# A split-precision transformer block on one core: the order of the weight products within a chunk

## The chip, the cores and the metric

The kernel runs on one NeuronCore of a Trainium2 chip. The metric is the device time of one execution in microseconds. Three executions of the kernel before took 2243.55, 2243.20 and 2241.29 us; their median is 2243.2 us.

## What is computed

Two transformer-like layers in sequence, over 256 tokens (the first with 16 meta tokens put ahead, 272 in all) and a model width of 2048, all in float32. Shortened from the reference:

```
# first block
h    = rms_norm(x, norm_g);  proj = h @ w_in            # 2048 x 12368 columns
y_a  = sparse attention (indexer, top-k) * silu(z_a)
y_b  = rms_norm(gated recurrence)       * silu(z_b)
x    = x + (sigmoid(gates) * (y @ w_branch)) summed over 2 branches @ w_out
# second block, modulated by mod = silu(c) @ ada_w + ada_b
h    = modulate(rmsnorm(x, norm1_g)); p = h @ w_in_2
y    = [neighbourhood attention, Fourier mix, long convolutions]
x    = x + g1 * (y @ w_out_2)
x    = x + g2 * ((gelu(conv(h2 @ w_gate)) * (h2 @ w_up)) @ w_down)
return rmsnorm(x, final_norm_g)
```

Nearly all the arithmetic is activations times large weight matrices (w_in, w_branch, w_out, w_in_2, w_out_2, ffn_w_up, ffn_w_down), each weight used once.

## The kernel before

The weights stream from memory into four buffers `raw`. ScalarE writes their upper part in fp32r (`whi`, line 561), VectorE the remainder (`wlo = raw - whi`, line 1104). Activations are split in the same way into a high and a low plane: `phi`/`plo` for most phases, `r_hi`/`r_lo` for phase FB, `y_hi`/`y_lo` for E, `c_hi`/`c_lo` for G and H, `o_hi`/`o_lo` for OA, `dhi`/`dlo` for M0 and M1. A full-precision product is then the sum of three fp32r products on TensorE, called a triple here: whi with the high plane, whi with the low plane, wlo with the high plane. Each of the three is one matmul instruction with a weight load (LDWEIGHTS) of its own.

The work is a list of units, each 256 output columns (for M0 and M1, all 1024 of a half), in phases FB, QB, IB, QI, K, KA, QA, VA, ZB, ZA, GA, GB, E, F, G, H, IH, IF, J, IQ, OA, OB, L, M0, M1. A unit is cut into chunks of 512 rows of the weight (four row tiles of 128, index `k4`; `kt` counts them over the unit), four chunks to most units. The function `chunk(c)` of TensorE (lines 1767 to 1830) issues one chunk's products; it waits once, at its start, for the chunk's `wlo` (semaphore `split_lo`), at the start of a unit for the banks to be evacuated (`gemm_free`), and its last product alone signals `mm`, on which ScalarE (which refills `whi`) and the evacuations wait. Unit u sums in banks 2p and 2p+1 of PSUM, p = u mod 2. There are three kinds:

- weights stationary, activations moving (lines 1785 to 1807; most phases): output columns on the partitions, in two halves `h` of 128, one bank each; the loop is h outside, k4 inside, then the triple. So twelve products in a row go to one bank, then twelve to the other. The moving operand has 256 columns, or 272 in FB, IB, KA, VA and the first half of K. In phase K the second half has only 16 stationary columns.
- DN, phases M0 and M1 (lines 1808 to 1819): activations stationary, 512 weight columns moving, one row tile to a chunk, four banks (two token halves `t`, two column halves `nb`); the bank changes after every triple.
- the rest, N2, phases H and J (lines 1820 to 1829): activations stationary, 256 weight columns moving, k4 outside, then t, then the triple; the bank changes after every triple.

Between chunks TensorE runs smaller work of the block (attention, recurrence, convolutions, transposes, the ada products), written out by hand at given chunk numbers.

Of the kernel before, what the change touches and what calls it, by code (L numbers as in the profile page):

```python
# [7 lines left out]
KT = D // 128  # L8
SEQ = 256
META = 16  # L10
T = META + SEQ
# [4 lines left out]
UC = 256  # L16
# [24 lines left out]
U0, NU, UNITS, C0, CHUNK = {}, {}, [], [], []  # L41
# [123 lines left out]
def program(nc, A, out):  # L165
# [5 lines left out]
    with ctx:  # L171
        top = [MEM]

        def at(name, shape, offset, dt=F32):
            return nc.alloc_sbuf_tensor_at(name, shape, dt, offset=4 * offset)
# [7 lines left out]
        def S(name):  # L183
            if name not in sems:
                sems[name] = ctx.enter_context(nc.semaphore(name))
            return sems[name]
# [17 lines left out]
        dhi = at("dhi", [128, 8, 256], base + 24576, F32R)  # L204
        dlo = at("dlo", [128, 8, 256], base + 26624, F32R)
# [11 lines left out]
        ps = [ctx.enter_context(nc.psum_tensor(f"ps{i}", [128, 512], F32)) for i in range(8)]  # L217
# [1546 lines left out]
        def _(pe):  # L1764
            mm = nc.tensor.matmul

            def chunk(c):

                u, q = CHUNK[c]
                name, kind, i = UNITS[u]  # L1770
                p = u % 2
                pe.wait_ge(S("split_lo"), c + 1)
                if kind == "DN":
                    j = u - U0["M0"]
                    if q == 0:
                        pe.wait_ge(S("dn_lo"), j + 1)
                elif q == 0 and u >= 2:

                    pe.wait_ge(S(f"gemm_free{p}"), (u - p) // 2)
                wh, wl = whi[c % 4], wlo[c % 4]  # L1780
                xh, xl = {"E": (y_hi, y_lo), "G": (c_hi, c_lo), "H": (c_hi, c_lo)}.get(name, (phi, plo))
                if name == "FB":
                    xh, xl = r_hi, r_lo
                if name == "OA":
                    xh, xl = o_hi[:, 4 * q:4 * q + 4, :], o_lo[q]
                if kind in ("Tall", "Tx", "T", "T8", "K", "BR"):
                    cc = {"Tall": slice(0, T), "Tx": slice(META, T), "K": slice(0, T)}.get(kind, slice(0, 256))
                    n = 144 if kind == "K" else UC
                    for h in range(2):
                        m = 16 if kind == "K" and h == 1 else 128  # L1790
                        if kind == "K" and h == 1:
                            cc = slice(META, T)
                        w = cc.stop - cc.start
                        b = 256 * (q // 2) if kind == "BR" else 0
                        o = ps[2 * p + h][0:m, b:b + w]
                        for k4 in range(4):
                            kt = 4 * q + k4
                            k = slice(n * k4 + 128 * h, n * k4 + 128 * h + m)
                            if u == 0 and h == 0:
                                pe.wait_ge(S("raw_lo"), kt + 1)  # L1800
                            st, en = kt == 0, c + 1 == C0[u + 1] and k4 == 3
                            if kind == "BR":
                                st, en = kt % 8 == 0, kt % 8 == 7
                            xk, yk = xh[:, k4 if name == "OA" else kt, cc], xl[:, k4 if name == "OA" else kt, cc]
                            mm(o, wh[:, k], xk, start=st, stop=False)  # L1805
                            mm(o, wh[:, k], yk, start=False, stop=False)  # L1806
                            l = mm(o, wl[:, k], xk, start=False, stop=en)  # L1807
                elif kind == "DN":
                    kd = 4 * p + q
                    for t in range(2):  # L1810
                        for nb in range(2):
                            o = ps[(4 if name == "M0" else 0) + 2 * t + nb][:, :]
                            k = slice(512 * nb, 512 * nb + 512)
                            xk = dhi[:, kd, 128 * t:128 * t + 128]
                            yk = dlo[:, kd, 128 * t:128 * t + 128]
                            st, en = i == 0 and q == 0, i == 10 and q == 3
                            mm(o, xk, wh[:, k], start=st, stop=False)  # L1817
                            mm(o, yk, wh[:, k], start=False, stop=False)  # L1818
                            l = mm(o, xk, wl[:, k], start=False, stop=en)  # L1819
                else:  # L1820
                    for k4 in range(4):
                        kt = 4 * q + k4
                        k = slice(UC * k4, UC * k4 + UC)
                        for t in range(2):
                            tt = slice(128 * t, 128 * t + 128)
                            o = ps[2 * p + t][:, 0:UC]
                            mm(o, xh[:, kt, tt], wh[:, k], start=kt == 0, stop=False)  # L1827
                            mm(o, xl[:, kt, tt], wh[:, k], start=False, stop=False)  # L1828
                            l = mm(o, xh[:, kt, tt], wl[:, k], start=False, stop=kt == KT - 1)  # L1829
                l.then_inc(S("mm"), 1)  # L1830

            def ada_tile(n):
# [107 lines left out]
            def attention(s):  # L1940

                c, odd = (s - S_NK) // 2, (s - S_NK) % 2
                if 1 <= c <= 13 and not odd:
                    chunk, w, _, _, _, pm = rope_of(c - 1)
                    if c == 1:
                        pe.wait_ge(S("rope_in"), 48)
                    if c - 1 < NNORM:
                        pe.wait_ge(S("nk_normed"), c)
                    if c >= 2:
                        pe.wait_ge(S("nk_turned"), c - 1)  # L1950
                    mm(ps[5][:, 0:w], pm, chunk, start=True, stop=True).then_inc(S("nk_rot"), 1)
# [49 lines left out]
            for c in slots("FB", "GB"):  # L2001
# [8 lines left out]
                u, q = CHUNK[c]  # L2010
                if (u, q) in TURN_AT:
                    to_tokens(TURN_AT[u, q])
                if u == U0["K"] + 1 and q == 0:
                    p = U0["K"] % 2
                    pe.wait_ge(S(f"gemm_free{p}"), evacuated(U0["K"], p))
                    pe.wait_ge(S("vt_tok"), 8)
                    for t in range(2):
                        l = nc.tensor.transpose(ps[6][:, 16 * t:16 * t + 16], wiT[0:16, 128 * t:128 * t + 128], ident[0:16, 0:16])
                    l.then_inc(S("wi_tp"), 1)
                recurrence(c)  # L2020
                if c == S_QN:
# [4 lines left out]
                    for j in range(16):  # L2026
                        l = mm(ps[6][:, j:j + 1], sqq[j // 4][:, 128 * (j % 4):128 * (j % 4) + 128], mean1[:, 0:1], start=True, stop=True)
# [174 lines left out]
            for c in slots("E", "OB"):  # L2202
                u, q = CHUNK[c]
                name, _, i = UNITS[u]
# [24 lines left out]
            for c in slots("L", "M1"):  # L2229
# [8 lines left out]
                kt = c - START["L"] - 8  # L2238
                if 0 <= kt < 16:
# [3 lines left out]
                    for t in range(2):  # L2243
                        l = nc.tensor.transpose(ps[4 + kt % 2][:, 128 * t:128 * t + 128], x1T[:, kt, 128 * t:128 * t + 128], ident[:, :])
# [129 lines left out]
```

## Time and profile before

| | |
|---|---|
| executions, us | 2243.55, 2243.20, 2241.29 (median 2243.2) |
| profiled execution, us | 2243.54 |
| its span, first to last instruction, us | 2241.7 |
| mean granted TensorE clock | 0.993 |
| busy: TensorE, its weight loads | 2186.1 us (98%), 2034.5 us (91%) |
| busy: VectorE, ScalarE | 1453.4 us (65%), 1028.9 us (46%) |
| matmuls and weight loads | 16534 each |

All from one profiled execution. Matmuls overlap in the pipeline: a record of 0.28 us stands every 0.12 us, so the time that one product costs is the distance from its start to the next one's start, and not its duration; busy time is the time that at least one is under way. In a window, the count in brackets includes those that started ahead of the window and end in it.

### The profile page before, as it was taken

The page shows a single profiled execution, that of the slowest core. Times are in us where ns is not written, and L with a number is a line of the kernel's source. Part 1 is how long each engine was busy: PE and PEld are TensorE (multiplying, and loading weights), DVE is VectorE, ACT ScalarE, POOL GpSimd, SP SyncE. Part 2 cuts the span into 40 slices and gives each one's busy share as a digit, 9 for nine tenths or more (in the row PEclk, how much of TensorE's full clock was granted, in tenths as well). Part 3 has the DMA queues.
Part 4 walks back from the last instruction along what each step waited for, and adds up shares of the span by engine and source line. Part 5 has one row for each costly group of instructions (what it writes and reads, how often), then busy time and mean ns, then how long its engine had stood idle before and what let it go on. Part 6 is the DMA issues. An engine that isn't in the chain of part 4 may idle for free.

```text
span 2241.7 us, 37995 instructions
## 1 busy us (share of the span) xinstructions
PE 2186.1 (98%) x16534; PEld 2034.5 (91%) x16534; DVE 1453.4 (65%) x1796; ACT 1028.9 (46%) x1394; POOL 6.2 (0%) x10
## 2 busy tenths in 40 slices
PE   7999999999999999999999999979999999999996
PEld 7989989878999999998888999979999999998885
DVE  7656546656757697696665677776666665555654
ACT  6453334334455555454433454454444443444453
POOL 0000000000000000000000000000000000000000
PEclk9999999999999999999999999989999999999998
DMA  9755655655447978786565756746676675555552
GB/s 318 248 197 192 190 190 172 205 194 176 145 150 256 314 232 266 252 279 221 181 206 155 239 165 206 244 166 233 223 237 233 228 233 188 182 190 199 189 191 92
DMA packets 344260, 469.55 MB, mean 209 GB/s; under 512 B 20445, under 2 KB 318301, under 8 KB 331102
## 3 DMA queue, kind: packets, MB, share of 16 engines
q1 hardware_dynamic: 344094, 467.12, 62.9%
q8 instruction: 130, 2.13, 0.4%
q14 instruction: 36, 0.29, 0.0%
HBM read 465.00 MB, written 2.10 MB: 208 GB/s over the span
## 4 chain that ended last, share of the span: by engine, by line
PE 94%; DVE 3%; ACT 2%; DMA 1%; issue 0%; SPq 0%; DVEq 0%; ACTq 0%
PE ps L1805 23%; PE ps L1807 22%; PE ps L1806 22%; PE ps L1819 4%; PE ps L1817 4%; PE ps L1818 4%; PE ps L1899 1%; PE ps L1828 1%; PE ps L1829 1%; PE ps L1827 1%; PE ps L1841 1%; ACT whi L561 1%; DVE wlo L1104 1%; PE ps L2176 1%; PE ps L2109 1%; PE ps L2103 1%
## 5 line engine op out<-in xcount | busy, mean ns | idle before, releaser
L1104 DVE TENSOR_TENSOR wlo<-raw,whi 128x1024 fp32r<-128x1024 f32 (+1 forms) x668 | 815.1, 1222 | 734.9 <-ACT whi L561 733.1
L561 ACT ACTIVATE whi<-raw 128x1024 fp32r<-128x1024 f32 (+1 forms) x668 | 705.2, 1056 | 1138.4 <-PE ps L1807 933.6
L1805 PE MATMUL ps<-phi,whi 128*128 128x256 f32 (+2 forms) x3744 | 1080.5, 289 | 7.5 <-DVE plo L1561 6.7
L1806 PE MATMUL ps<-plo,whi 128*128 128x256 f32 (+2 forms) x3744 | 1056.1, 282 | 0.0
L1807 PE MATMUL ps<-phi,wlo 128*128 128x256 f32 (+2 forms) x3744 | 1055.7, 282 | 0.0
L1805 PEld LDWEIGHTS ps<-phi,whi 128*128 128x128 f32 (+1 forms) x3744 | 707.5, 189 | 40.9 <-issue 30.2
L1806 PEld LDWEIGHTS ps<-plo,whi 128*128 128x128 f32 (+1 forms) x3744 | 704.8, 188 | 7.2 <-issue 6.0
L1807 PEld LDWEIGHTS ps<-phi,wlo 128*128 128x128 f32 (+1 forms) x3744 | 708.2, 189 | 0.3
L1170 DVE SCALAR_TENSOR_TENSOR arena<-raw,cst,arena 128x1024 f32<-128x1024 f32 x120 | 153.6, 1280 | 3.5 <-DVE arena L1251 0.5
L1817 PE MATMUL ps<-whi,dhi 128*128 128x512 f32 x352 | 136.9, 389 | 0.0
L1819 PE MATMUL ps<-wlo,dhi 128*128 128x512 f32 x352 | 136.9, 389 | 0.0
L1818 PE MATMUL ps<-whi,dlo 128*128 128x512 f32 x352 | 136.9, 389 | 0.0
L1818 PEld LDWEIGHTS ps<-whi,dlo 128*128 128x128 f32 x352 | 66.1, 188 | 13.8
L1819 PEld LDWEIGHTS ps<-wlo,dhi 128*128 128x128 f32 x352 | 66.1, 188 | 13.7
L1817 PEld LDWEIGHTS ps<-whi,dhi 128*128 128x128 f32 x352 | 66.1, 188 | 13.6
L1805 PE MATMUL ps<-y_hi,whi 128*128 128x256 f32 x256 | 72.1, 282 | 0.0
L1806 PE MATMUL ps<-y_lo,whi 128*128 128x256 f32 x256 | 71.8, 280 | 0.0
L1807 PE MATMUL ps<-y_hi,wlo 128*128 128x256 f32 x256 | 71.6, 280 | 0.0
L1805 PE MATMUL ps<-r_hi,whi 128*128 128x272 f32 x128 | 38.8, 303 | 12.1 <-DVE wlo L1104 12.1
L1806 PEld LDWEIGHTS ps<-y_lo,whi 128*128 128x128 f32 x256 | 48.2, 188 | 0.0
L1807 PEld LDWEIGHTS ps<-y_hi,wlo 128*128 128x128 f32 x256 | 48.2, 188 | 0.0
L1805 PEld LDWEIGHTS ps<-y_hi,whi 128*128 128x128 f32 x256 | 48.0, 187 | 0.0
(347 smaller groups left out, 2324.4 us busy)
## 6 DMA issues: line engine op xcount, KB each, us to landing
raw<-w_in_dram SPq DMA_DIRECT2D x151, 1024.0 KB, 6.2
raw<-ada_w_dram SPq DMA_DIRECT2D x96, 1024.0 KB, 5.0
raw<-ffn_w_up_dram SPq DMA_DIRECT2D x88, 1024.0 KB, 5.1
raw<-ffn_w_down_dram SPq DMA_DIRECT2D x44, 1024.0 KB, 5.2
raw<-w_out_dram SPq DMA_DIRECT2D x32, 1024.0 KB, 5.7
raw<-w_branch_dram SPq DMA_DIRECT2D x16, 1024.0 KB, 6.5
arena<-xT_dram SPq DMA_DIRECT2D x4, 544.0 KB, 6.9
arena<-ctxT_dram SPq DMA_DIRECT2D x1, 2048.0 KB, 10.5
```

Source lines behind the costliest of these rows:

```text
L561: nc.scalar.activation(whi[c % 4][:, 0:w], src, ACT.Copy).then_inc(S("split_hi"), 1)
L1104: v.tensor_tensor(wlo[c % 4][:, 0:w], src, whi[c % 4][:, 0:w].bitcast(F32), ALU.subtract).then_inc(S("split_lo"), 1)
L1170: t = v.scalar_tensor_tensor(total, x, by, R(ADA_SUM[n - 1][half], 1024), ALU.mult, ALU.add)
L1805: mm(o, wh[:, k], xk, start=st, stop=False)
L1806: mm(o, wh[:, k], yk, start=False, stop=False)
L1807: l = mm(o, wl[:, k], xk, start=False, stop=en)
L1817: mm(o, xk, wh[:, k], start=st, stop=False)
L1818: mm(o, yk, wh[:, k], start=False, stop=False)
L1819: l = mm(o, xk, wl[:, k], start=False, stop=en)
L1827: mm(o, xh[:, kt, tt], wh[:, k], start=kt == 0, stop=False)
L1828: mm(o, xl[:, kt, tt], wh[:, k], start=False, stop=False)
L1829: l = mm(o, xh[:, kt, tt], wl[:, k], start=False, stop=kt == KT - 1)
```

## The change

In all three kinds, the loop over the banks becomes the innermost. For each row tile the first term of the triple (whi, high plane) is issued to every bank of the unit in turn, then the second term (whi, low plane) to every bank, then the third (wlo, high plane). No two products in a row write the same bank any more. The same products are issued with the same operands, each with its own weight load; in each bank the terms are added in the same order. The waits, the signal `mm` on the chunk's last product and the start and stop flags of each bank stay; for unit 0 the wait for `raw_lo` now stands ahead of six products of a row tile in place of three. In the first kind, terms one and two shared their stationary slice of `whi`; now no two neighbours share one, and instead the moving plane is the same in each pair (the two halves `h`). In DN neighbours that differ in `nb` alone now share the stationary tile. In N2 the moving slice of the weights is the same in each pair (the two `t`); before, terms one and two shared it.

```diff
--- before.py
+++ after.py
@@ -1783,50 +1783,40 @@
                     xh, xl = r_hi, r_lo
                 if name == "OA":
                     xh, xl = o_hi[:, 4 * q:4 * q + 4, :], o_lo[q]
+
                 if kind in ("Tall", "Tx", "T", "T8", "K", "BR"):
                     cc = {"Tall": slice(0, T), "Tx": slice(META, T), "K": slice(0, T)}.get(kind, slice(0, 256))
                     n = 144 if kind == "K" else UC
-                    for h in range(2):
-                        m = 16 if kind == "K" and h == 1 else 128
-                        if kind == "K" and h == 1:
-                            cc = slice(META, T)
-                        w = cc.stop - cc.start
-                        b = 256 * (q // 2) if kind == "BR" else 0
-                        o = ps[2 * p + h][0:m, b:b + w]
-                        for k4 in range(4):
-                            kt = 4 * q + k4
-                            k = slice(n * k4 + 128 * h, n * k4 + 128 * h + m)
-                            if u == 0 and h == 0:
-                                pe.wait_ge(S("raw_lo"), kt + 1)
-                            st, en = kt == 0, c + 1 == C0[u + 1] and k4 == 3
-                            if kind == "BR":
-                                st, en = kt % 8 == 0, kt % 8 == 7
-                            xk, yk = xh[:, k4 if name == "OA" else kt, cc], xl[:, k4 if name == "OA" else kt, cc]
-                            mm(o, wh[:, k], xk, start=st, stop=False)
-                            mm(o, wh[:, k], yk, start=False, stop=False)
-                            l = mm(o, wl[:, k], xk, start=False, stop=en)
+                    b = 256 * (q // 2) if kind == "BR" else 0
+                    for k4 in range(4):
+                        kt = 4 * q + k4
+                        if u == 0:
+                            pe.wait_ge(S("raw_lo"), kt + 1)
+                        st, en = kt == 0, c + 1 == C0[u + 1] and k4 == 3
+                        if kind == "BR":
+                            st, en = kt % 8 == 0, kt % 8 == 7
+                        xi = k4 if name == "OA" else kt
+                        for x, wx, first, last in ((xh, wh, st, False), (xl, wh, False, False), (xh, wl, False, en)):
+                            for h in range(2):
+                                m = 16 if kind == "K" and h == 1 else 128
+                                tt = slice(META, T) if kind == "K" and h == 1 else cc
+                                k = slice(n * k4 + 128 * h, n * k4 + 128 * h + m)
+                                l = mm(ps[2 * p + h][0:m, b:b + tt.stop - tt.start], wx[:, k], x[:, xi, tt], start=first, stop=last)
                 elif kind == "DN":
                     kd = 4 * p + q
-                    for t in range(2):
-                        for nb in range(2):
-                            o = ps[(4 if name == "M0" else 0) + 2 * t + nb][:, :]
-                            k = slice(512 * nb, 512 * nb + 512)
-                            xk = dhi[:, kd, 128 * t:128 * t + 128]
-                            yk = dlo[:, kd, 128 * t:128 * t + 128]
-                            st, en = i == 0 and q == 0, i == 10 and q == 3
-                            mm(o, xk, wh[:, k], start=st, stop=False)
-                            mm(o, yk, wh[:, k], start=False, stop=False)
-                            l = mm(o, xk, wl[:, k], start=False, stop=en)
+                    st, en = i == 0 and q == 0, i == 10 and q == 3
+                    for x, wx, first, last in ((dhi, wh, st, False), (dlo, wh, False, False), (dhi, wl, False, en)):
+                        for t in range(2):
+                            for nb in range(2):
+                                l = mm(ps[(4 if name == "M0" else 0) + 2 * t + nb][:, :], x[:, kd, 128 * t:128 * t + 128],
+                                       wx[:, 512 * nb:512 * nb + 512], start=first, stop=last)
                 else:
                     for k4 in range(4):
                         kt = 4 * q + k4
                         k = slice(UC * k4, UC * k4 + UC)
-                        for t in range(2):
-                            tt = slice(128 * t, 128 * t + 128)
-                            o = ps[2 * p + t][:, 0:UC]
-                            mm(o, xh[:, kt, tt], wh[:, k], start=kt == 0, stop=False)
-                            mm(o, xl[:, kt, tt], wh[:, k], start=False, stop=False)
-                            l = mm(o, xh[:, kt, tt], wl[:, k], start=False, stop=kt == KT - 1)
+                        for x, wx, first, last in ((xh, wh, kt == 0, False), (xl, wh, False, False), (xh, wl, False, kt == KT - 1)):
+                            for t in range(2):
+                                l = mm(ps[2 * p + t][:, 0:UC], x[:, kt, 128 * t:128 * t + 128], wx[:, k], start=first, stop=last)
                 l.then_inc(S("mm"), 1)
 
             def ada_tile(n):
```

## Rows read from the trace of the kernel before

**Rows 1.** The page: busy time by engine; granted clock in 40 slices.

```profile
PE 2186.1 (98%) x16534; PEld 2034.5 (91%) x16534; DVE 1453.4 (65%) x1796; ACT 1028.9 (46%) x1394; POOL 6.2 (0%) x10
...
PEclk9999999999999999999999999989999999999998
```

**Rows 2.** The page: the chain that ended last, by engine and by line.

```profile
PE 94%; DVE 3%; ACT 2%; DMA 1%; issue 0%; SPq 0%; DVEq 0%; ACTq 0%
PE ps L1805 23%; PE ps L1807 22%; PE ps L1806 22%; PE ps L1819 4%; PE ps L1817 4%; PE ps L1818 4%; PE ps L1899 1%; PE ps L1828 1%; PE ps L1829 1%; PE ps L1827 1%; PE ps L1841 1%; ACT whi L561 1%; DVE wlo L1104 1%; PE ps L2176 1%; PE ps L2109 1%; PE ps L2103 1%
```

**Rows 3.** Waits of TensorE, the longest: us in total, times, longest.

```profile
PE ps L1805 <- DVE wlo L1104: 12.1, 1, 12.1
```

**Rows 4.** Groups by line: xcount | busy us, mean ns | idle before.

```profile
L1805 PE MATMUL ps<-phi,whi 128*128 128x256 f32 (+2 forms) x3744 | 1080.5, 289 | 7.5 <-DVE plo L1561 6.7 <-DVE plo L1697 0.8
...
L1817 PE MATMUL ps<-whi,dhi 128*128 128x512 f32 x352 | 136.9, 389 | 0.0
...
L1805 PE MATMUL ps<-r_hi,whi 128*128 128x272 f32 x128 | 38.8, 303 | 12.1 <-DVE wlo L1104 12.1
...
L1827 PE MATMUL ps<-whi,c_hi 128*128 128x256 f32 x128 | 36.2, 283 | 0.0
```

**Rows 5.** Windows, TensorE alone: stretch, us, busy (xproducts), granted clock, DMA share, GB/s.

```profile
744.40:789.60 45.20, 45.20 (x386) 1.00 0.92 317
801.40:835.90 34.50, 34.50 (x290) 1.00 0.82 266
...
954.60:977.60 23.00, 23.00 (x194) 1.00 0.87 288
977.60:1023.70 46.10, 46.10 (x386) 1.00 0.84 280
1570.20:1831.40 261.20, 261.20 (x2210) 1.00 0.68 230
1985.40:2224.40 239.00, 239.00 (x1056) 1.00 0.50 174
```

**Rows 6.** Timeline, phase L: start us, duration; 24 products of one chunk, of which five.

```profile
1750.89 0.28 PE L1805 MATMUL ps<-phi,whi 128*128 128x256 f32 x1
1751.00 0.28 PE L1806 MATMUL ps<-plo,whi 128*128 128x256 f32 x1
1751.12 0.28 PE L1807 MATMUL ps<-phi,wlo 128*128 128x256 f32 x1
1751.24 0.28 PE L1805 MATMUL ps<-phi,whi 128*128 128x256 f32 x1
...
1753.73 0.28 PE L1805 MATMUL ps<-phi,whi 128*128 128x256 f32 x1
```

**Rows 7.** Timeline, phase J: first product of a chunk and what follows its 24th.

```profile
1151.98 0.28 PE L1827 MATMUL ps<-whi,phi 128*128 128x256 f32 x1
...
1154.82 0.59 PE L2109 MATMUL ps<-arena 128*128 128x512 f32 x1
```

**Rows 8.** Timeline, phase H: the bank changes at every L1827.

```profile
984.96 0.28 PE L1828 MATMUL ps<-whi,c_lo 128*128 128x256 f32 x1
985.08 0.28 PE L1829 MATMUL ps<-wlo,c_hi 128*128 128x256 f32 x1
985.20 0.28 PE L1827 MATMUL ps<-whi,c_hi 128*128 128x256 f32 x1
```

**Rows 9.** Timeline, phase M0: the bank changes at every L1817.

```profile
2051.55 0.39 PE L1818 MATMUL ps<-whi,dlo 128*128 128x512 f32 x1
2051.78 0.39 PE L1819 MATMUL ps<-wlo,dhi 128*128 128x512 f32 x1
2052.01 0.39 PE L1817 MATMUL ps<-whi,dhi 128*128 128x512 f32 x1
```

**Rows 10.** Timeline, the first products, at half clock.

```profile
12.92 0.43 PE L1805 MATMUL ps<-r_hi,whi 128*128 128x272 f32 x1
...
14.28 0.43 PE L1805 MATMUL ps<-r_hi,whi 128*128 128x272 f32 x1
```

## The prediction

> **What bounds the kernel.** First the page's busy times: TensorE is under way 98% of the span, VectorE 65%, ScalarE 46%, and the clock is granted in full in all but two of 40 slices [rows 1]. But a matmul record of 0.28 us stands every 0.12 us [rows 6], so 98% says only that a product is always in the pipe, not that the array is at its peak. Then the chain of waits: 94% of it is TensorE, and 82% the nine lines of `chunk` that the change rewrites [rows 2]. The longest wait of TensorE is its start, 12.1 us [rows 3]. So it's the distance from one product's start to the next that makes the time, and a nanosecond of it on all products counts in full. ScalarE and VectorE have slack of 54% and 35%: a TensorE faster by a few per cent would still be fed.
>
> How many products: phi as the moving operand has 3744 triples, FB 128, H 128 [rows 4]; G, OA and J have 128 each as H has, E 256, M0 and M1 together 352 [rows 4]. That is 4512 + 128 + 352 = 4992 triples, 14,976 products. 1200 of them have 272 columns (12 units of 96, and half of K), 1056 have 512, 48 are K's small ones, which leaves 12,672 of 256 columns.
>
> What one costs, from the windows (count less the two already under way at the window's start, one in M0/M1) [rows 5]:
> - L, units 8 to 30: 2208 in 261.2 us, 118.3 ns
> - E, first four units: 384 in 45.2 us, 117.7 ns; E, last three: 288 in 34.5 us, 119.8 ns, as good as 120
> - G: 192 in 23.0 us, 119.8 ns. H: 384 in 46.1 us, 120.1 ns
> - M0 and M1 (512 columns): 1055 in 239.0 us, 226.5 ns
>
> **What is there to gain.** H and M0 differ by 256 columns and 106.4 ns, so 0.416 ns a column, the array's 2.4 GHz; 256 columns are 106.5 ns, and each product carries 11.8 ns (L) to 13.6 ns (H) on top. In the first products, at the 1.2 GHz level, six of 272 columns take 1.36 us [rows 10], 0.833 ns a column, and nothing on top. Whatever the 12 to 14 ns are, they show only at full clock. The change helps if they are a stall of a product that adds to sums which its forerunner has just written.
>
> **The bank in the trace of before.** The old code has both cases side by side. In H the bank changes after each triple. The steps are: from term one to two and from two to three (same bank), 0.12 us; from term three to the next triple's first (another bank), 0.12 us [rows 8]; here three rows of 16 alike. A stall in the two same-bank steps would make the third one shorter. In M0 the same: 0.23 us within the bank and 0.23 us at the change [rows 9]. A buffer ahead of the array could smear such a stall over a triple; but G changes its bank after twelve products and H after three, with the same planes c_hi and c_lo: 119.8 and 120.1 ns [rows 5]. Were the bank to matter, H, with a third of its steps going to another bank, would be well below G. L and J give the same answer on phi and plo: one chunk of L is 24 products in 2.84 us (of 1750.89 to 1753.73) [rows 6], one chunk of J with the change at each third product is 24 in 2.84 us (1151.98 to 1154.82) [rows 7]: 118.3 ns both. So I take the bank's worth as zero.
>
> **The change part by part.**
> - Instructions: 14,976 products and their loads before, as many after. TensorE issues each with a load of its own; in the old order terms one and two of the first kind share the stationary slice and yet L1806 has its own load, as the page's equal counts of matmuls and loads say [rows 1]. Nothing is saved or added: 0.
> - Order of operands, the second effect of the edit. In the first kind, six products of a row tile now stand together where three did, the moving plane repeats in neighbours, and the stationary slice no longer does. J has this outer order already (k4 outside, the two banks inside) and runs at L's 118.3 ns [rows 6, 7]: 0. Bounds: the pace isn't one number, it lies between 117.7 ns (early E) and 120.1 ns (H) in undisturbed windows [rows 5], though the columns, the clock and the kind of loads are the same. The 1056 products of G, H and late E are at the slow pace already, the other 11,616 at 118.3 or thereabouts. All at 120.0: 1.7 ns x 11,616 = +19.7 us. All at 117.7: 0.6 x 11,616 + 2.3 x 1056 = -9.4 us. I take 0, as L and J are the nearest rows.
> - M0 and M1: the four banks in turn, with stationary slices repeating in pairs. 226.5 ns is 512 columns at 0.416 plus 13.5, at a bank change and without; 0, bounds as for the second rival and the first.
> - K's small second half (16 columns of weights) is mixed with the large half: 96 products; even 2 ns each is 0.2 us.
> - Waits. `split_lo`, `gemm_free` and `mm` stand where they stood, at a chunk's first and last product, so ScalarE's refill of `whi` and the evacuations are released at the same point. Unit 0 waits for `raw_lo` before each row tile; now six products lie between two such waits in place of three, so it can only wait less, and there is no gap there today, only the 12.1 us for the first `wlo` [rows 3], which stays. 0.
> - Clock: TensorE stays continuously busy as before, so its grant stays at 2.4 GHz: 0.
>
> Sum against the profiled execution: 2243.5 + 0 = 2243.5 us; it stands 0.3 above the median of the runs. I forecast 2243.3.
>
> The Trainium skill has a rule on the point, in Perfetto Trace Analysis, Optimizing Tensor Performance: independent groups should rotate through banks so that evacuations overlap, and one accumulation group stays in one bank by construction. It gives no reason to rotate within a group's sums; here TensorE doesn't wait for evacuations, so by this rule too the sum is unchanged.
>
> **Rivals.**
> 1. The stall is real and hidden from the comparisons above. If all that stands on top of the columns went, it would be 11.8 x 11,616 + 13.5 x (1056 + 1056) + about 13 x 1200 = 137 + 29 + 16 = -182 us, 2062 us. For it: the fixed part exists, and twelve in a row to one bank is what most phases do. Against: G and H, L and J, and the steps inside H and M0. A partial effect would be at least some tens of us. Chance 0.06.
>  The Trainium skill, TensorE: Matmul & The Clock Gate, Back-to-back issue gap, gives N/2.4 + 2.5 ns between warm matmuls: 109.2 ns at 256 columns and 215.8 at 512. No row here comes that low. If the new order reached it, my estimate from that section of the Trainium skill is 9.1 ns x 11,616 and about 10.7 ns on the others, some -140 us, 2103 us; it is a case of this rival and within its chance.
> 2. The pace locks at the slow value. In L the step from term one to two, where the stationary slice repeats, is the short one (1750.89 to 1751.00, 0.11 us), the other two are 0.12 [rows 6]. If loading the same slice again is what saves there, the new order, in which no neighbours share a slice in the first kind, loses it, and all go at 120.0: +19.7 us, 2263 us. For it: E went from 117.7 to 120 within the phase with nothing changed in its operands [rows 5], so small things tip the pace. Against: G repeats the slice as well and is at 120 [rows 5]; J has no repeated stationary slice and is at 118.3. It decides from 0.35 ns per product on (4.5 us / 12,672). Chance 0.22.
> 3. The pace shifts the other way, as in early E: down to 2234 us. For it: a repeated moving plane could ease the fetch; against: J's neighbours share theirs too and gain nothing. Chance 0.15.
> 4. Forecast, no change beyond 0.2%: 0.57.
>
> **How the numbers follow.** A measurement of this kernel can tell about 0.2%, 4.5 us, from nothing. Faster: rivals 1 and 3, 0.06 + 0.15 = 0.21. Slower: 0.22. Same: 0.57. Range: rivals 2 and 3 with the forecast are 0.94 and span 2234 to 2263; I leave out rival 1, and give 2232 to 2264 for the spread of single runs of 2 us.
>
> **What would show it.** Right: windows of L at 118.3, G and H at 120, M0 at 226.5 ns per product; loads and matmuls 16534 each. Rival 1: windows of L near 107 to 110 ns, TensorE's waits for `wlo` growing as its feeders come late. Rival 2: L at 120.0 and all three steps of a triple alike. Rival 3: G or H below 119. The prediction is wrong at its root if H and G, which now have the same bank rotation, part from each other, or if both fall together.

## The result, and the profile after

The changed kernel takes 2229.7 us (median of five, 2229.3 to 2230.9) against 2243.2 us before: ratio 0.9942, 95% interval 0.9931 to 0.9953. That is 13.5 us or 0.6% less. The forecast was no change, and the measured time lies 2.3 us below the stated range.

The page after: busy times, granted clock, chain by engine and by line (line 1804 is the product of the first kind, 1811 that of M0 and M1, 1819 that of H and J).

```profile
PE 2171.2 (97%) x16534; PEld 2019.3 (91%) x16534; DVE 1453.3 (65%) x1796; ACT 1029.0 (46%) x1394; POOL 6.3 (0%) x10
...
PEclk9999999999999999999999999989999999999998
...
PE 94%; DVE 4%; ACT 2%; issue 0%; DMA 0%; SPq 0%; DVEq 0%; ACTq 0%
PE ps L1804 67%; PE ps L1811 11%; PE ps L1819 4%; PE ps L1889 1%; PE ps L1831 1%; DVE wlo L1104 1%; ACT whi L561 1%; PE ps L2166 1%; PE ps L2099 1%; PE ps L2093 1%; PE ps L2061 1%; PE ps L1941 1%; PE ps L1958 0%; PE ps L2053 0%; PE ps L1979 0%
```

The counts are those of [rows 1], and the chain is that of [rows 2]: still TensorE, product after product. No wait of TensorE over 1 us went away or came; the longest is again 12.1 us for the first `wlo`. The row of clock digits is the same too, but a digit 9 says only 90% or more, and one short stretch hides behind it. Three us of products shortly after a 2.9 us wait in phase IB, in the kernel before, in this one, and in the run e1_neworder_onebank described below, which has the new order of operands:

```profile
131.00:134.00 3.00, 3.00 (x16) 0.52 0.64 223
...
130.00:133.00 3.00, 3.00 (x27) 1.00 0.59 210
...
130.00:133.00 3.00, 3.00 (x15) 0.50 0.67 237
```

The granted clock was at its lower level there before and in e1, and stayed at 2.4 GHz in the profiled execution of the changed kernel. IB took 70.5 us before, 70.3 in e1 and 68.7 here: so 1.6 us of the difference between the two profiles is a drop of the clock that didn't come this time, and not the order. The rest of the gain must be in the distance between products.

Windows of TensorE after, as in [rows 5]: two units of G, all of H, units 8 to 30 of L, and units 1 to 10 of M0 with M1 up to its last unit (units are counted from 0). A count includes the two products already under way (one in M0).

```profile
948.30:971.30 23.00, 23.00 (x194) 1.00 0.86 288
971.40:1017.40 46.00, 46.00 (x386) 1.00 0.83 279
...
1561.00:1819.20 258.20, 258.20 (x2210) 1.00 0.69 233
...
1982.30:2199.80 217.50, 217.50 (x961) 1.00 0.52 182
```

G: 192 in 23.0 us, H: 384 in 46.0, 119.8 ns both, as before. M0 and M1: 960 in 217.5, 226.6 ns, as before. L: 2208 in 258.2 us, 116.9 ns, against 118.3 in [rows 5]. The sum by phase, from the start of a phase's first product to that of the next phase's, before and after:

| phases | change, us |
|---|---|
| L (4224 products) | -5.7 |
| GA, GB, F, IQ, OB, IH, IF | -4.4 |
| FB, IB, KA, VA (272 columns) | -2.9, of which 1.6 is IB's clock |
| QB, QI, QA, ZB, ZA | -1.0 |
| E | +0.2 |
| G, H, J, OA, K, M0, M1 | -0.2 |

Together 14.0 us of the span, 12.4 of them without IB's clock. So the gain is in those phases, all of the first kind, whose moving operand lies in a plane with 272 columns to a row tile (`phi`, `plo`, `r_hi`, `r_lo`). The phases with 256 columns to a row tile (G, OA, E) got the same new order of banks and gained nothing, and H, J, M0 and M1 nothing either. K, one unit with planes of 272 columns, gained nothing as well.

### The profile page after: what moved, and what is told of

Its sections match the earlier page's. It is cut to its first block, busy times and chain, and to the rows that moved or that the text cites. A ratio compares the mean times of both kernels' runs of the same rounds, so it can differ in the third digit from the quotient of the medians.

```text
span 2227.8 us, 37995 instructions
## 1 busy us (share of the span) xinstructions
PE 2171.2 (97%) x16534; PEld 2019.3 (91%) x16534; DVE 1453.3 (65%) x1796; ACT 1029.0 (46%) x1394; POOL 6.3 (0%) x10
## 4 chain that ended last, share of the span: by engine, by line
PE 94%; DVE 4%; ACT 2%; issue 0%; DMA 0%; SPq 0%; DVEq 0%; ACTq 0%
PE ps L1804 67%; PE ps L1811 11%; PE ps L1819 4%; PE ps L1889 1%; PE ps L1831 1%; DVE wlo L1104 1%; ACT whi L561 1%; PE ps L2166 1%; PE ps L2099 1%; PE ps L2093 1%; PE ps L2061 1%; PE ps L1941 1%; PE ps L1958 0%; PE ps L2053 0%; PE ps L1979 0%
## 5 line engine op out<-in xcount | busy, mean ns | idle before, releaser
L1804 PE MATMUL ps<-phi,whi 128*128 128x256 f32 (+2 forms) x3744 | 775.3, 288 | 7.7 <-DVE plo L1561 6.8
L1804 PE MATMUL ps<-plo,whi 128*128 128x256 f32 (+2 forms) x3744 | 744.9, 280 | 0.0
L1804 PE MATMUL ps<-phi,wlo 128*128 128x256 f32 (+2 forms) x3744 | 743.9, 280 | 0.0
L1804 PEld LDWEIGHTS ps<-phi,whi 128*128 128x128 f32 (+1 forms) x3744 | 573.4, 188 | 48.1 <-issue 36.2
L1804 PEld LDWEIGHTS ps<-plo,whi 128*128 128x128 f32 (+1 forms) x3744 | 571.5, 188 | 0.5
L1804 PEld LDWEIGHTS ps<-phi,wlo 128*128 128x128 f32 (+1 forms) x3744 | 571.4, 188 | 0.5
L1170 DVE SCALAR_TENSOR_TENSOR arena<-raw,cst,arena 128x1024 f32<-128x1024 f32 x120 | 153.5, 1280 | 3.5 <-DVE arena L1251 0.5
L1811 PE MATMUL ps<-whi,dhi 128*128 128x512 f32 x352 | 94.1, 389 | 0.0
L1811 PE MATMUL ps<-whi,dlo 128*128 128x512 f32 x352 | 94.1, 389 | 0.0
L1811 PE MATMUL ps<-wlo,dhi 128*128 128x512 f32 x352 | 94.1, 389 | 0.0
L1889 PEld LDWEIGHTS ps<-arena 128*128 128x128 f32 x256 | 31.2, 191 | 9.9 <-issue 6.7
```

Source lines behind the costliest of these rows:

```text
L1170: t = v.scalar_tensor_tensor(total, x, by, R(ADA_SUM[n - 1][half], 1024), ALU.mult, ALU.add)
L1804: l = mm(ps[2 * p + h][0:m, b:b + tt.stop - tt.start], wx[:, k], x[:, xi, tt], start=first, stop=last)
L1811: l = mm(ps[(4 if name == "M0" else 0) + 2 * t + nb][:, :], x[:, kd, 128 * t:128 * t + 128], wx[:, 512 * nb:512 * nb + 512], start=first, ...
L1889: x = mm(ps[4 + g % 2][:, 128 * (h - h0):128 * (h - h0) + 128], kk, qq, start=True, stop=True)
```

## The experiments

**Bank and order taken apart.** Two runs make the other two corners of a square whose corners are the old and the new kernel. In e1_neworder_onebank the operands come in the new order, but a row tile's six products go to one bank. Both edits touch the first kind alone (without phase K), mix the sums of the two halves, and so don't compute the reference's output; the work is the same. Shortened:

```diff
-  l = mm(ps[2 * p + h][0:m, b:b + tt.stop - tt.start], wx[:, k], x[:, xi, tt], start=first, stop=last)
+  o = ps[2 * p + (h if kind == "K" else k4 % 2)][0:m, b:b + tt.stop - tt.start]
+  l = mm(o, wx[:, k], x[:, xi, tt], start=f, stop=z and wx is wl and (h == 1 or kind == "K"))
```

> The new order of the operands, but in the first kind all six products of a row tile go to one bank (row tiles take the two banks in turn), so five steps of six stay in the same bank; M0, M1, H and J as in the changed kernel. The sums of the two column halves are mixed, so the output isn't the reference's; the work on every engine is the same. Theory A, the bank doesn't matter and the order of the operands gives the gain: 2229.7 us as the changed kernel, within 2. Theory B, the stall of two products in a row on one bank gives the gain: back to 2241 to 2243 us, or above.

2230.1 us (2229.8 to 2231.1), 0.9945 of before, 0.9933 to 0.9958. Units 8 to 30 of L:

```profile
1562.60:1820.80 258.20, 258.20 (x2210) 1.00 0.69 233
```

The same window length as after, 258.2 us. In e2_oldorder_altbank the operands come in the old order, and the bank changes with every product:

```diff
-  mm(o, wh[:, k], xk, start=st, stop=False)
-  mm(o, wh[:, k], yk, start=False, stop=False)
-  l = mm(o, wl[:, k], xk, start=False, stop=en)
+  for t, (wx, x) in enumerate(((wh, xk), (wh, yk), (wl, xk))):
+      o = ps[2 * p + ((12 * h + 3 * k4 + t) % 2 if alt else h)][0:m, b:b + w]
+      l = mm(o, wx[:, k], x, start=f, stop=...)
```

> The old order of the operands, but in the first kind the bank changes with every product; M0, M1, H and J as before. Sums mixed as in the run above, the work the same. Theory A: 2242.5 us as the kernel before, within 2. Theory B: 2230 us or less.

2242.3 us (2241.0 to 2243.4), 0.9998, 0.9989 to 1.0007; L:

```profile
1570.10:1831.30 261.20, 261.20 (x2210) 1.00 0.68 230
```

261.2 us, as in [rows 5] to the tenth. The bank is worth nothing that shows; the order of the operands is worth the gain, some 12 us between these two runs. So the rotation of banks, for which the change was made, is not what makes the kernel faster.

**Which part of the order.** e3_tile_outside puts the row tile outside and leaves the triple inside, so that of the three things that the new order changes only one is left: six products of a row tile stand together.

```diff
-  for x, wx, first, last in ((xh, wh, st, False), (xl, wh, False, False), (xh, wl, False, en)):
-      for h in range(2):
+  for h in range(2):
+      for x, wx, first, last in ((xh, wh, st, False), (xl, wh, False, False), (xh, wl, False, en)):
```

> Row tile outside, then the half, then the triple (J's nesting) in the first kind: six products of a row tile together as in the changed kernel, three in a row to a bank, the stationary slice repeated in terms one and two, no moving plane repeated in neighbours but at the change of half. If the gain comes from six products per row tile standing together: 2230 us. If it comes from the moving plane that repeats in neighbours (or from the stationary slice that no longer does): 2242 us. Theory B: at least 4 us of the gain are there, since one step in three now changes the bank: 2238 us or less.

2232.0 us (2230.3 to 2232.3), 0.9951, 0.9939 to 0.9964; L at the pace of the new order:

```profile
1563.40:1821.60 258.20, 258.20 (x2210) 1.00 0.69 233
```

So in L neither the repeated moving plane nor the stationary slice that no longer repeats counts; it is how long the stream stays on one row tile. The new kernel is 2.3 us ahead of this one; some 0.9 us of it is E, where this order gives 120.1 ns and the new one 118.9, and in the profiles another 1.6 us is IB's clock, which is low in this run as in e1.

**Why the row tile.** A row tile of `phi` is 272 columns, 1088 bytes, further on than the last: 64 bytes modulo 256. By the kernel's own layout, and taking addresses modulo 256, the slices of `whi` and `wlo` start at 128 (outside phase K), the row tiles of `phi` and `plo` at 128, 192, 0, 64 in turn, those of `c_hi` and `c_lo` always at 128, those of `y_hi` at 128 and of `y_lo` at 192. (Phases that leave out the 16 meta tokens start 64 bytes later in each row tile of `phi` and `plo`.) e4_bench puts blocks of 192 products with nothing around them behind the last unit (shortened):

```diff
+ for o, w, x, st, en in bench("old", "real", 256, 48, 48):    # order, banks, step in columns, starts
+     mm(o, w, x, start=st, stop=en)                           # ... 16 such blocks
```

> The changed kernel with 16 blocks of 192 extra products each behind the last unit, written to banks 4 and 5 and read by nobody; the output stays the reference's. Blocks differ in order (old, new, row tile outside), in banks (as in the kernel, alternating with every product, one for 24), in the step between row tiles of the moving planes (272, 256, 264, 288, 320 columns) and in where the planes start. Span: some 16 x 22.7 = 363 us more. Theory A: block 1 (old, 272 columns) 118.3 ns a product, block 2 (new, 272) 117.2, block 3 (old, banks alternating) 118.3, block 4 (new, one bank) 117.2; with a step of 256 columns 120.0 in both orders, as in G and H, so the place of the moving operand in memory sets the pace. Theory B: block 3 as fast as block 2 and block 4 as slow as block 1; blocks with 256 columns faster in the new order than in the old.

The windows of fourteen of the blocks, each from its first product to the next block's first:

```profile
2211.08:2233.80 22.72, 22.72 (x193) 1.00 0.23 93
2233.80:2256.27 22.47, 22.47 (x194) 1.00 0.00 1
2256.27:2278.98 22.71, 22.71 (x194) 1.00 0.01 1
2278.98:2301.45 22.47, 22.47 (x194) 1.00 0.00 1
2301.45:2323.90 22.45, 22.45 (x194) 1.00 0.01 1
2323.90:2346.92 23.02, 23.02 (x194) 1.00 0.00 1
2346.92:2369.96 23.04, 23.04 (x194) 1.00 0.01 1
2369.96:2392.58 22.62, 22.62 (x194) 1.00 0.00 1
2392.58:2415.36 22.78, 22.78 (x194) 1.00 0.01 1
2415.36:2437.15 21.79, 21.79 (x194) 1.00 0.00 1
2437.15:2459.77 22.62, 22.62 (x194) 1.00 0.01 1
2459.77:2482.28 22.51, 22.51 (x194) 1.00 0.00 1
...
2504.93:2527.75 22.82, 22.82 (x194) 1.00 0.00 1
2527.75:2550.47 22.72, 22.72 (x194) 1.00 0.01 1
```

In ns a product (length / 192), for the rows in turn: old order 118.3; new 117.0; old with alternating banks 118.3; new in one bank 117.0; row tile outside 116.9. Then a step of 256 columns: at 128 (distance 0 from the weights) old 119.9, new 120.0; and in the old order at 192, 0, 64: 117.8, 118.6, 113.5. The pace goes by the place, over 6.5 ns, and at the one fixed place tried in both orders the order is worth nothing. That also is G and OA: planes at 128, 120 ns in either order. Where the place changes, the order counts again: with the high plane at 128 and the low one at 192, as in E, old 117.8 and new 117.2; with a step of 288 columns (row tiles at 128 and 0 in turn) old 118.9, new 118.3. These lie below the means of the fixed paces, 119.3 in both cases, so a mix is not simply its parts. A step of 320 columns is 1280 bytes, five times 256, and in the last block, from the starts of its products, gives 120.0 as 256 columns do.

e5_bench_places moves the weights as well, and swaps the roles (shortened):

```diff
+ bench("first", 256, 0, 16), (..., 16, 16), (..., 32, 16), (..., 48, 16)     # weights 64 bytes further on
+ bench("n2", 256, 0), ..., bench("n2", 256, 0, 0, 512), ...                  # weights moving, as in H and M0
```

> Again the changed kernel with blocks of 192 extra products behind the last unit. In the run e4_bench the pace went by where the moving operand starts, in bytes modulo 256: 128 gave 120.0 ns, 192 gave 117.8, 0 gave 118.7, 64 gave 113.4 (step of 256 columns, weights at 128). Theory A1, the start of the moving operand alone decides: with the weights moved on by 64 bytes the four places 128, 192, 0, 64 give the same four paces again. Theory A2, the distance between moving operand and weights decides: the four paces come back one place later, the best (113.4) with the planes at 128. Blocks with the activations stationary and 256 or 512 weight columns moving (as H, J, M0, M1; moving at 128, planes at 128, 192, 0, 64): under A1 all alike, 120 and 226.7; under A2 they differ by up to 6 ns. 272 columns: spread of some ns likewise. A row tile used for 12 products in place of 6 (step 272): below 117.0 if each change of row tile costs, the mean of the four paces, 117.4, if not.

```profile
2211.25:2233.86 22.61, 22.61 (x193) 1.00 0.23 93
2233.86:2256.90 23.04, 23.04 (x194) 1.00 0.00 1
2256.90:2279.52 22.62, 22.62 (x194) 1.00 0.01 1
2279.52:2302.29 22.77, 22.77 (x194) 1.00 0.00 1
2302.29:2325.32 23.03, 23.03 (x194) 1.00 0.01 1
2325.32:2347.94 22.62, 22.62 (x194) 1.00 0.00 1
2347.94:2370.73 22.79, 22.79 (x194) 1.00 0.01 1
2370.73:2393.34 22.61, 22.61 (x194) 1.00 0.00 1
2393.34:2436.90 43.56, 43.56 (x194) 1.00 0.00 1
2436.90:2481.70 44.80, 44.80 (x193) 1.00 0.00 1
2481.70:2526.31 44.61, 44.61 (x193) 1.00 0.00 0
2526.31:2570.28 43.97, 43.97 (x193) 1.00 0.00 1
...
2712.16:2733.95 21.79, 21.79 (x194) 1.00 0.01 2
2733.95:2756.60 22.65, 22.65 (x194) 1.00 0.00 1
```

Distance here is the place of the activation planes less that of the weights, whichever of them moves. Rows 1 to 4, weights at 192, moving operand at 128, 192, 0, 64: 117.8, 120.0, 117.8, 118.6 ns. The slow 120.0 came along to 192: it stands where both are at the same place, so for three of the four distances the distance decides, not the place (A2). But the fast pace did not come along: at distance -64 it was 113.5 with the weights at 128, and is 117.8 here. With the weights at 128 and the planes at 64 it came again in this same execution: the row at 2712.16, in the new order, 113.5. Rows 5 to 8, weights moving and activations stationary at 128, 192, 0, 64: 119.9, 117.8, 118.7, 117.8, the same values with the roles swapped, but for the fast one. Rows 9 to 12, 512 columns at the four places: 226.9, 233.3, 232.3, 229.0; there distance 0 is the best, not the worst. The last row, 272 columns a step with 12 products to a row tile: 118.0. In it the places 128 and 192 come five times for three of 0 and 64, and the mean of the fixed paces weighted so is (5 x 120.0 + 5 x 117.8 + 3 x 118.6 + 3 x 113.5) / 16 = 117.8. The 0.2 ns to it leave no room for a large price of a change of row tile.

**The place changed in the kernel.** e6_planes_moved lays `phi` and `plo` out with 256 columns to a row tile from phase F on, all at 64:

```diff
+ phi6 = at("phi6", [128, KT, 256], top[0] - 2 * KT * T + 48, F32R)
+ plo6 = at("plo6", [128, KT, 256], top[0] - KT * T + 48, F32R)
- xh, xl = {...}.get(name, (phi, plo))
+ xh, xl = {...}.get(name, (phi6, plo6) if u >= U0["F"] else (phi, plo))
```

> The changed kernel, but from phase F on phi and plo are laid out with 256 columns to a row tile in place of 272 and start 192 bytes further on, so that every row tile starts at 64 bytes modulo 256. Nothing else moves. If the place of the moving operand sets the pace: the 6912 products of F, IH, IF, IQ, OB and L go from 117.0 to 113.4 ns, -25 us, 2205 us. If the pace depends on something else and the blocks at the end of the kernel were a special case: 2230 us.

2224.0 us (2220.9 to 2226.9), 0.9918, 0.9904 to 0.9932: a gain on the new kernel, but a quarter of what I expected. Units 1 to 4 of OB, units 8 to 30 of L, units 34 to 43 of L:

```profile
1410.00:1431.70 21.70, 21.70 (x194) 1.00 0.83 282
1558.80:1818.80 260.00, 260.00 (x2210) 1.00 0.68 231
1858.30:1967.00 108.70, 108.70 (x962) 1.00 0.61 202
```

OB: 192 in 21.7 us, 113.0 ns; L at first 2208 in 260.0, 117.8 ns; at its end 960 in 108.7, 113.2 ns. The operands, the step and the order are the same in both parts of L. e7_planes_moved_old_order is the same edit on the kernel before:

> The same new place of the planes in the kernel before, with its old order. If the order matters only through the row tiles that start at different places: L as fast as in e6_planes_moved, 113.4 ns, and the total 2242.4 - 6912 x 5.0 ns = 2208 us; what is left to the new order is the first block, 4 to 6 us. If the order has a worth of its own (1.3 ns on each product): 2217 us.

2226.5 us (2223.9 to 2228.1), 0.9928, 0.9914 to 0.9941:

```profile
1412.40:1434.20 21.80, 21.80 (x194) 1.00 0.83 283
1561.20:1821.20 260.00, 260.00 (x2210) 1.00 0.68 231
1860.70:1969.40 108.70, 108.70 (x962) 1.00 0.61 203
```

Both numbers that I gave were missed, since L ran at 117.8 ns for most of its length, but the question is answered: with every row tile at one place the old order is as fast as the new in L (260.0 and 108.7 us in both), the bank never changing within twelve products. In the profiles e6 is 3.6 us ahead in the first block, whose planes are untouched, and 1.1 us behind in the second.

e8_all_planes_moved adds `top[0] += 48` ahead of the arena, so that the other planes lie at 64 too (only `y_lo` at 128):

> As e6_planes_moved, and the arena with the planes of E, G, H, OA, M0 and M1 192 bytes further on as well, so that c_hi, c_lo, o_hi, o_lo, y_hi, dhi and dlo start at 64 modulo 256 and y_lo at 128. The 768 products of G and OA go from 120.0 to 113.4 ns, -5 us against e6_planes_moved: 2200 us; E (768) between 0 and -5 us more. H, M0 and M1 have the weights moving, which stay where they are: unchanged if the place of the moving operand alone decides, else up to 6 ns a product either way, -9 to +9 us.

2218.4 us (2217.8 to 2219.8), 0.9894, 0.9881 to 0.9908; far from the 2200 expected, as e6 was already. Two units of G, H, units 8 to 30 of L, and M0 with M1:

```profile
945.90:967.60 21.70, 21.70 (x194) 1.00 0.85 283
967.70:1011.10 43.40, 43.40 (x386) 1.00 0.92 303
...
1550.00:1810.00 260.00, 260.00 (x2210) 1.00 0.68 231
...
1969.20:2188.90 219.70, 219.70 (x961) 1.00 0.53 180
```

G 192 in 21.7 us and H 384 in 43.4: 113.0 ns in place of 119.8, in H with the stationary operand moved alone; within the chunks E came to 117.1 and OA to 116.0. M0 and M1 lose: 228.9 ns, from 226.6. The other way round, e9_planes_same_place has the planes of `phi` at 128, the place of the weights:

> As e6_planes_moved, but the planes of phi and plo start at 128 modulo 256, the place of the weights: distance 0 for every row tile from phase F on. If the distance between moving operand and weights sets the pace: the 6912 products go from the changed kernel's 117.2 to 120.0 ns, +19 us, 2249 us, slower than the kernel before, with the banks in turn as in the changed kernel. If the bank rotation had any worth of its own, or if 256 columns to a row tile were what helped in e6_planes_moved: 2230 us or less.

2250.0 us (2248.3 to 2252.4), 1.0036, 1.0023 to 1.0048; slower than before, as expected, with L at 120.0 ns:

```profile
1569.30:1834.20 264.90, 264.90 (x2210) 1.00 0.67 227
```

**Two paces with the same operands.** Units 1 to 5 of F in e8, and in e10_nudge_16, whose kernel differs from e8's only further on, in L:

```profile
843.60:898.00 54.40, 54.40 (x483) 1.00 0.82 271
...
840.40:896.90 56.50, 56.50 (x482) 1.00 0.80 262
```

480 products at 113.3 ns in one and 117.7 in the other: the same instructions with the same layout, in two executions. So the pace isn't fixed by the program alone, and a single execution can mislead by 2 us or so. In e6 to e8 L runs at 117.8 ns for 23 units, and from unit 34 on at 113.3; the change comes in units 31 to 33, where the small products for the gate g2 stand between the chunks. e10_nudge_16 and e11_nudge_128 take e8 and add one product that nobody reads at the start of each of the units 6 to 30:

```diff
+ if name == "L" and q == 0 and 6 <= i <= 30:
+     mm(ps[6][:, 0:128], wh[:, 0:128], phi6[:, 0, 0:128], start=True, stop=True)
```

> e8_all_planes_moved with one extra product of 16 columns, read by nobody, at the start of each of the units 6 to 30 of L. In e8_all_planes_moved these units run at 117.8 ns and the last ten at 113.3 with the same operands; if the pace is a state that holds until something disturbs the stream, and the nudge is such a thing: some or all of the 2400 products go to 113.3, up to -10 us + 25 x 0.05, 2209 us. If the pace is set by something else that goes on beside (transfers, the other engines): 2219.5 us, units 6 to 30 still at 117.8.

2220.3 us (2217.2 to 2224.3), 0.9903, 0.9888 to 0.9917: units 6, 10, 14, 18, 22, 26 and 30 ran at 113.5 ns, all the others at 117.7 or 117.8. In the total it isn't distinct from e8, and so lies at the expectation for no effect, though the units do show one; in its profile the slow F costs 2.5 us.

> The same with an extra product of 128 columns: 2210 us if it shifts the state, 2220 us if not.

2215.8 us (2215.0 to 2219.0), 0.9884, 0.9869 to 0.9899. Units 6, 7, 8 and 9:

```profile
1527.30:1538.31 11.01, 11.01 (x100) 1.00 0.48 160
1538.31:1549.73 11.42, 11.42 (x100) 1.00 0.83 280
1549.73:1560.74 11.01, 11.01 (x100) 1.00 0.57 188
1560.74:1572.16 11.42, 11.42 (x100) 1.00 0.84 284
```

11.01, 11.42, 11.01 and 11.42 us for 96 products and the extra one: the steps within the chunks are 113.5 and 117.8 ns in turn, and so on up to unit 30. Each extra product throws the stream from one pace to the other. The total lies between the two that were expected, since half the units stay slow. e12_nudge_once keeps only the one at unit 6 (`i == 6`):

> e8_all_planes_moved with a single extra product of 128 columns, at the start of unit 6 of L. In e11_nudge_128, with one at each unit's start, the pace went 113.5, 117.8, 113.6, 117.8 and so on from unit 6, so each one throws the stream from one state to the other. If a state holds until it is disturbed, one product at unit 6 leaves units 6 to 30 all at 113.3: 25 x 96 x 4.4 ns = 10 us less than e8_all_planes_moved, 2208 to 2211 us. If the alternation in e11_nudge_128 had another cause, such as the two pairs of banks: 2214 to 2219 us.

2209.2 us (2207.1 to 2211.6), 0.9854, 0.9837 to 0.9870; units 8 to 30:

```profile
1548.50:1798.70 250.20, 250.20 (x2210) 1.00 0.71 241
```

2208 in 250.2 us, 113.3 ns: after that one product the pace held for all 23 units of the window, as expected, so neither the parity of the unit nor its pair of banks makes the two paces. This version is faster than both kernels, by 1.5% and by 0.9%.

## Why the prediction was wrong

- **What bounds it: right.** The chain and the waits are as before, and the time went with the distance between products. That a product's pace is not one number held too.
- **The bank is worth zero: right.** It was read from G against H and from the steps inside H and M0, and e1 and e2 show it: 2230.1 with one bank, 2242.3 with alternating ones. Rival 1 is out. That no wait or load would change was right too. The clock was put at 0 from slices that show only 90% or more; behind them lies the drop in IB, 1.6 us in one profile and not in the other, which has nothing to do with the order.
- **The order of the operands at 0: wrong, and this is the step that failed.** I took J's pace as the nearest row, since J already has the row tile outside. But in J the weights move, always from one place, and `phi` is the stationary operand; the new order gains in the phases in which `phi` moves. J stayed at its pace, L went from 118.3 to 116.9 ns, and the order of the operands, forecast at 0, is worth some 12 us (e1 against e2). At the row tile at 64 J's steps stay at 117.8 ns, before and after, where L's come down to 113.3 (below); why, with the same two places, isn't shown. The comparison L against J answered for the bank and I let it answer for the nesting as well.
- **The bounds: too tight below.** The low end was 117.7 ns, early E, the fastest undisturbed window that I had looked at, and I applied it to the whole of the kernel: at most -9.4 us, where the order gave some -12. The new order runs L at 116.9; 3.0 us over 2208 products is 1.36 ns each, on 4224 products of L the 5.7 us, and the other phases with 272-column row tiles give the rest. A row at 113 ns was not in the long windows of before, since no phase stayed at distance -64.
- **Rival 3 had the right sign, its reason was wrong.** A pace that shifts down, 15%; I blamed the repeated moving plane, and e3, which has it only where the half changes, keeps L's gain. Rival 2, the short step that would be lost with the repeated slice, did not come. The sign that I named for being wrong at the root, G and H parting or falling together, couldn't show this failure: their planes lie at one place, and both stayed at 119.8.
- **What the gain is.** The mean steps from one product to the next, in L, units 8 to 30, put down to the row tile of the first of the two, for the row tiles at 128, 192, 0, 64: before 118.1, 117.4, 118.7, 119.2 ns; after 117.8, 117.8, 116.9, 115.3. Alone these places give 120.0, 117.8, 118.6, 113.5. On the row tile at 64 the three steps of before are 118.1, 120.0, 119.4 ns, and the six of after 121.7, 115.8, 114.2, 113.3, 113.3, 113.3: with six at a time the pace comes down after three products, and this row tile has the larger part of the gain. That with three at a time the stream leaves too early for it fits, but is argued. The row tile at 0 gains 1.8 ns and ends below its own pace alone; why is open, and so is why the whole runs at 116.9, under the mean of the four, 117.5.

The Trainium skill, TensorE: Matmul & The Clock Gate, says in its section Step-by-step: what each phase is for, that matmul and weight load read SBUF through two independent ports, so that loading the next weights takes nothing from the running matmul. By that rule one wouldn't expect the place of one operand against the other to matter. The runs show that it does, up to 6.5 ns of 120 (e4, e5, e8), with either operand moved. The gap of N/2.4 + 2.5 ns in its section Back-to-back issue gap, 109.2 at 256 columns, which it calls that of an isolated matmul, was reached nowhere here; the lowest steady pace is 113.3.

What stays open: what in the chip makes the distance between the two addresses count; why distance -64 has two steady paces and which disturbance leads to which; whether it has the fast one at all when the weights lie elsewhere than at 128; and why distances that help at 256 columns cost at 512. Other weights' places weren't tried beyond the two of e4 and e5. Nor are two paces confined to -64: E, with its planes at 128 and 192, ran before at 117.7 and then 119.8 ns within the phase [rows 5], and after at 118.9, where the block with the same places and the new order took 117.2.

## What to carry to other kernels

When the array is always busy and the chain is one product after another, measure the pace per product phase by phase and ask why it differs between phases with the same shapes: here two planes that differed only in their layout ran at 118 and 120 ns, and laying out those two anew, in the old order, was worth as much (0.7%, e7) as the reordering (0.6%); both, with the other planes moved too, gave 1.1% (e8). A row of one kind of loop answers for another only in what the two have in common: name for each comparison which operand moves. And to judge an edit that changes two things at once (bank and order), make the two kernels that change one each, even with sums that mean nothing.

## What the runs showed of the hardware that was not expected

- The distance between the two operands' addresses (activation planes less weights), modulo 256 bytes, changes the pace at full clock, whichever of them moves: at 256 fp32r columns 120.0 ns at distance 0, 117.8 at +64, 118.6 at 128, and 113.3 or 117.8 at -64 (e4, e5); at 512 columns 226.6 at 0 and 228.9 to 233.3 elsewhere (M0 and M1, e5, e8).
- With the weights at 128 and the planes at 64 the stream has two steady paces, 113.3 and 117.8 ns. Each held for as long as it was undisturbed (23 units, 250 to 260 us), and one extra product of 128 columns switched it at every unit from 7 to 30, 24 times in a row; one of 16 columns led to the fast pace in one unit of four. The fast pace was seen steady at these two places alone, with the planes moving (F, G, OB, L) and with the weights moving (H); at distance -64 with the weights at 192 one block ran, at 117.8.
- Adding to the sums just written costs nothing that shows: 258.2 us for 2208 products with five steps of six in one bank as with none.
